# Output projection of block 1: seven products in place of eight, with the sums of its weights on GpSimd

## The reference

```python
def first_block(x, w_in, attn_sinks, conv_w, w_branch_a, w_branch_b, w_branch_c, w_out,
                ln1_g, ln1_b, w_ffn_gate, w_ffn_up, w_ffn_down, ln2_g, ln2_b):
    for l in range(DEPTH):
        mix = hybrid_mixer(x, w_in[l], attn_sinks[l], conv_w[l], w_branch_a[l],
                           w_branch_b[l], w_branch_c[l], w_out[l])
        x = layer_norm(ALPHA * x + mix, ln1_g[l], ln1_b[l])
        ffn = swiglu(x, w_ffn_gate[l], w_ffn_up[l], w_ffn_down[l])
        x = layer_norm(ALPHA * x + ffn, ln2_g[l], ln2_b[l])
    return x
```

## Time and profile before

| | |
|---|---|
| median of three runs | 2504.95 us (2500.95, 2504.95, 2506.22) |
| the profiled execution | 2509.21 us, span of its profile 2507.3 us |
| granted TensorE clock, mean over the span | 0.960 |
| TensorE matmuls busy | 2206.5 us (88%) |
| VectorE busy | 1181.2 us (47%) |
| ScalarE busy | 366.2 us (15%) |
| GpSimd busy | 38.5 us (2%), 69 instructions |
| HBM over the span | 262 GB/s |

### The profile page before, as it was taken

The page is one execution under the profiler, slowest core; times in us unless marked ns, Lnnn a source line. Parts: engine busy times, 40 slices in busy tenths (PEclk is TensorE's granted clock), DMA queues, the critical chain, the costliest instruction groups (busy, mean ns, idle before and its releaser), DMA issues.

```text
span 2507.3 us, 43433 instructions
## 1 busy us (share of the span) xinstructions
PE 2206.5 (88%) x19414; PEld 1567.8 (63%) x19414; DVE 1181.2 (47%) x2135; ACT 366.2 (15%) x818; POOL 38.5 (2%) x69
## 2 busy tenths in 40 slices
PE   8999999999999999999999988888799986555564
PEld 7898699488987984746545645454488643232322
DVE  6776477687755875935533221222435631111111
ACT  1121000012210000234521000000201520000000
POOL 0000000000000010000000000000000000000000
PEclk9999999999999999999998999999999998888877
DMA  8655755476558564511327999999921189999996
GB/s 318 223 167 200 242 183 213 154 252 236 168 185 268 169 222 162 199 45 36 118 111 331 418 427 426 426 427 425 377 103 34 71 339 425 427 426 428 427 427 282
DMA packets 168411, 659.15 MB, mean 263 GB/s; under 512 B 8326, under 2 KB 55938, under 8 KB 143522
## 3 DMA queue, kind: packets, MB, share of 16 engines
q1 hardware_dynamic: 162544, 639.66, 65.5%
q0 software_dynamic: 5312, 16.57, 2.1%
q10 hardware_dynamic: 370, 0.15, 0.0%
HBM read 655.12 MB, written 1.23 MB: 262 GB/s over the span
## 4 chain that ended last, share of the span: by engine, by line
PE 61%; DMA 29%; DVE 7%; ACT 2%; issue 1%; DVEq 0%; SPq 0%; ACTq 0%
PE psum L2291 21%; DMA ring<-in_moe_w_up 10%; DMA ring<-in_moe_w_gate 9%; DMA ring<-in_moe_w_down 9%; PE psum L789 5%; PE psum L2459 4%; PE psum L538 4%; PE psum L2236 3%; PE psum L2349 3%; PE psum L715 3%; PE psum L603 2%; PE psum L601 2%; PE psum L806 2%; PE psum L2467 1%; PE psum L2312 1%; PE psum L859 1%
## 5 line engine op out<-in xcount | busy, mean ns | idle before, releaser
L789 PE MATMUL psum<-ring,arena 128*32 128x256 f32 x5888 | 382.7, 416 | 161.8 <-DMA ring<-in_moe_w_up 87.3
L789 PEld LDWEIGHTS psum<-ring,arena 128*32 128x32 f32 x5888 | 207.8, 118 | 333.5 <-issue 138.3
L806 PE MATMUL psum<-ring,lnp 128*32 128x256 f32 x3072 | 193.9, 407 | 71.0 <-DMA ring<-in_moe_w_down 66.5
L1649 DVE TENSOR_TENSOR arena<-psum,spare 32x512 f32<-32x512 f32 (+1 forms) x128 | 70.9, 554 | 363.5 <-PE psum L806 362.2
L806 PEld LDWEIGHTS psum<-ring,lnp 128*32 128x32 f32 x3072 | 104.3, 116 | 158.4 <-DMA ring<-in_moe_w_down 50.5
L1638 DVE TENSOR_TENSOR lnp<-arena,psum 128x512 f32<-128x512 f32 (+1 forms) x32 | 26.1, 815 | 331.3 <-PE psum L789 331.3
L2291 PE MATMUL psum<-ht,ring 128*128 128x128 f32 x1408 | 168.2, 279 | 4.4 <-DMA ring<-in_w_in 3.4
L2291 PEld LDWEIGHTS psum<-ht,ring 128*128 128x128 f32 x1408 | 163.3, 195 | 8.4 <-issue 8.4
L538 PE MATMUL psum<-ring,ht 128*128 128x512 f32 x320 | 140.6, 595 | 0.0
L1096 ACT ACTIVATE arena<-psum 128x512 f32<-128x512 f32 (+1 forms) x32 | 15.7, 490 | 674.0 <-PE psum L789 674.0
L2693 DVE SCALAR_TENSOR_TENSOR spare<-ring,arena,spare 128x512 f32<-128x512 f32 x168 | 113.4, 743 | 0.0
(11 more groups left out here) (517 smaller groups left out, 3175.0 us busy)
## 6 DMA issues: line engine op xcount, KB each, us to landing
ring<-in_moe_w_down SPq DMA_DIRECT2D x64, 2048.0 KB
ring<-in_moe_w_gate SPq DMA_DIRECT2D x62, 2048.0 KB
ring<-in_moe_w_up SPq DMA_DIRECT2D x60, 2048.0 KB
ring<-in_w_in SPq DMA_DIRECT2D x52, 1024.0 KB
ring<-in_ada_w SPq DMA_DIRECT2D x48, 1024.0 KB
ring<-in_w_ffn_gate SPq DMA_DIRECT2D x22, 1024.0 KB
ring<-in_w_ffn_up SPq DMA_DIRECT2D x22, 1024.0 KB
ring<-in_w_ffn_down SPq DMA_DIRECT2D x20, 1024.0 KB
```

Source lines behind the costliest of these rows:

```text
L789: last = mm(bank[32 * j:32 * j + 32, SPLIT * m:SPLIT * m + SPLIT], (x_last if layer else x_four)[:, k, e % 4, SLOTS * m:SLOTS * m + SLOTS] ...
L806: last = mm(bank[32 * j:32 * j + 32, SPLIT * m:SPLIT * m + SPLIT], hidT[:, e % 2, a:a + 32], slot[:, f % 4, SPLIT * j:SPLIT * j + SPLIT], ...
L1649: ins = TTo(y_four[32 * q:32 * q + 32, s0:, cols], view(bank[r, 0:width], len(src), SPLIT), gb_moe[r, s0:, cols], ALU.mult)
```

## The change

The projection is taken as seven block products. With rows of `merged` (transposed) split in two halves of the inner dimension and tokens in two tiles, a11, a21, a12, a22 are blocks of 128 partitions x 4 x 128, and b11, b21, b12, b22 those of w_out, 4 x 512 columns each.

- TensorE: seven products of four calls, in the order 1, 6, 5, 2, 3, 7, 4, each with a bank; waits for the sums it needs.
- VectorE: four sums of `merged` blocks (128x512) after the merge. The assembly of the down projection is made into functions (`first_half`, `second_half`) and used for both; the weight sums of the first FFN panel now stand between the halves, behind a wait for GpSimd's last subtraction.
- GpSimd: four subtractions of w_out blocks (128x2048). They are queued ahead of the layer norm's parameter loads, wait for both w_out panels, for branch a's product (whose tiles they overwrite), for the merge of gate a, and the fourth for the last transpose of attention c.
- ScalarE: copies products 1 and 5 out of PSUM; the copy of `adaG` moves ahead of the first product of FFN panel 7 (counted from 0).
- Both w_out panels are released at the projection's end, where the first was released half way.

```diff
-    layer += [("wo", 0, 0), ("wo", 0, 1), R, ("wo", 1, 0), ("wo", 1, 1), R]
+    layer += [("wo", c) for c in SEVEN] + [R, R]
...
-        part_5 = ht[:, 3072:3584]
+        part_5 = [arena[:, 4608:5120], ht[:, 3072:3584]]
+        out_left = {5: view(arena[:, 3072:3584], 4, P), 6: view(arena[:, 3584:4096], 4, P), 3: view(arena[:, 4096:4608], 4, P)}
+        out_right = {6: view(ht[:, 2048:4096], 4, HALF), 7: view(arena[:, 10752:12800], 4, HALF), 4: view(arena[:, 0:2048], 4, HALF)}
...
+                for n_panel in (OUT_PANEL, OUT_PANEL + 1):
+                    pool.wait_ge(panel_in[n_panel % RING], l * (32 * LAYER_PANELS // RING) + 32 * (n_panel // RING + 1))
+                w1, w2 = (view(ring[:, n % RING, :], KT, HALF) for n in (OUT_PANEL, OUT_PANEL + 1))
+                b11, b21, b12, b22 = w1[:, 0:4, :], w1[:, 4:8, :], w2[:, 0:4, :], w2[:, 4:8, :]
+                sub = nc.gpsimd.tensor_tensor
+                pool.wait_ge(pe_done, banks.full("layer", ("ma", 3), l))
+                sub(out_right[7], b22, b12, ALU.subtract).then_inc(out_right_ready, 1)
+                pool.wait_ge(out_right_ready, 4 * l + 1)
+                sub(b12, b12, b11, ALU.subtract).then_inc(out_right_ready, 1)
+                pool.wait_ge(out_right_ready, 4 * l + 2)
+                pool.wait_ge(gate_a_merged, l + 1)
+                sub(out_right[6], b22, b12, ALU.subtract).then_inc(out_right_ready, 1)
+                pool.wait_ge(out_right_ready, 4 * l + 3)
+                pool.wait_ge(pe_done, banks.full("layer", ("ptc", 7), l))
+                sub(out_right[4], b21, out_right[6], ALU.subtract).then_inc(out_right_ready, 1)
                 pool.wait_ge(pe_done, banks.full("layer", ("sv", FIRST["ff"] - 1, "D"), l))
...
-                for n in range(2):
-                    project([("wo", n, 0), ("wo", n, 1)], panel(l, HALF), merged)
+                b1, b2 = panel(l, HALF), panel(l, HALF)
+                for c in SEVEN:
+                    bank = open_bank(pe, "layer", ("wo", c), l)
+                    if c in (5, 6, 3, 7):
+                        pe.wait_ge(out_left_ready, 4 * l + {5: 1, 6: 2, 3: 3, 7: 4}[c])
+                    if c in (7, 5, 6, 4):
+                        pe.wait_ge(out_right_ready, 4 * l + {7: 1, 5: 2, 6: 3, 4: 4}[c])
+                    for k in range(4):
+                        a = P * (c in (4, 7))
+                        left = out_left[c][:, k, :] if c in out_left else merged[:, 4 * (c in (2, 4)) + k, a:a + P]
+                        whole = b2 if c in (3, 5) else b1
+                        right = out_right[c][:, k, :] if c in out_right else whole[:, 4 * (c in (2, 3)) + k, :]
+                        last = mm(bank, left, right, start=k == 0, stop=k == 3)
+                    last.then_inc(pe_done, 1)
...
+                for c, part in ((1, part_1), (5, part_5[0])):
+                    take(("wo", c), part, part=HALF)
                 root(0, 0)
...
                 for p in range(PAIRS):
+                    if p == 7:
+                        take(("adaG",), ada_g, part=SEQ)
                     first_product(FIRST["ff"] + p)
...
+                            elif kind == "a" and m == 3:
+                                ins.then_inc(gate_a_merged, 1)
+                                dve.wait_ge(gate_a_merged, l + 1)
...
+                dve.wait_ge(merged_ready, l + 1)
+                a11, a21, a12, a22 = (merged[:, 4 * n:4 * n + 4, P * r:P * r + P] for n in range(2) for r in range(2))
+                TTo(out_left[5], a21, a22, ALU.add).then_inc(out_left_ready, 1)
+                dve.wait_ge(out_left_ready, 4 * l + 1)
+                TTo(out_left[6], out_left[5], a11, ALU.subtract).then_inc(out_left_ready, 1)
+                dve.wait_ge(out_left_ready, 4 * l + 2)
+                TTo(out_left[3], a12, out_left[6], ALU.subtract).then_inc(out_left_ready, 1)
+                TTo(a21, a11, a21, ALU.subtract).then_inc(out_left_ready, 1)
...
-                add_residual([("wo", 0, 0), ("wo", 0, 1)])
-                for t in range(TT):
-                    stats(t, (0,))
+                def first_half(kind):
+
+                    wait_emptied(dve, "layer", (kind, 1), l)
+                    scaled(x00, part_1)
+                    plus((kind, 6), part_12, part_1)
+                    for xs in (x01, x10, x11):
+                        scaled(xs, part_12)
+
+                def second_half(kind, n, loaded, done):
+
+                    wait_emptied(dve, "layer", (kind, 5), l)
+                    for xs in (x01, x11):
+                        step(TTo(xs, xs, part_5[n], ALU.add))
+                    plus((kind, 2), x00, x00)
+                    stats(0, (0,))
+                    plus((kind, 3), x01, x01)
+                    stats(0, (1,))
+                    layer_norm(n, 0, loaded, done)
+                    plus((kind, 7), x11, x11, last=False)
+                    stats(1, (1,))
+                    plus((kind, 7), x10, x10)
+                    plus((kind, 4), x10, x10)
+                    stats(1, (0,))
+                    layer_norm(n, 1, loaded, done)
+
+                first_half("wo")
+                dve.wait_ge(out_right_ready, 4 * l + 4)
                 weight_sums(FIRST["ff"])
-                add_residual([("wo", 1, 0)])
-                stats(0, (1,))
-                layer_norm(0, 0, ln1_loaded, x1_ready)
-                add_residual([("wo", 1, 1)])
-                stats(1, (1,))
-                layer_norm(0, 1, ln1_loaded, x1_ready)
+                second_half("wo", 0, ln1_loaded, x1_ready)
                 dve.wait_ge(x1_ready, 2 * l + 2)
```

More of the change, by code:

```diff
@@ L1895, in program @@
     LAYER_PANELS = banks.stage_panels["layer"][1]
-    ADA_PANELS, DOWN_PANEL = (5, 8, 13, 17, 21, 34), 39
+    ADA_PANELS, OUT_PANEL, DOWN_PANEL = (5, 8, 13, 17, 21, 34), 22, 39
     SEVEN_PANELS = (0, 1, 2, 6, 7, 10, 11, 14, 15, 18, 19, 27, 28, 29, 30, 31, 32, 33, 35, 36, 37, 38)
@@ L2032, in program @@
         gate_ready = sem("gate_ready")
+        gate_a_merged = sem("gate_a_merged")
+        out_left_ready, out_right_ready = sem("out_left_ready"), sem("out_right_ready")
         hid_sums_ready, w_sums_ready = sem("hid_sums_ready"), sem("w_sums_ready")
@@ L2587, in _ @@
                     A(ff[:, 0], ff[:, 0], ACT.Silu).then_inc(sil_ready, 1)
-                    if p == 7:
-                        take(("adaG",), ada_g, part=SEQ)
                 act.wait_ge(ctx_ms_ready, l + 1)
                 A(st[:, 4:6], st[:, 4:6], ACT.Sqrt).then_inc(ctx_rms_ready, 1)
-                for n, part in ((1, part_1), (5, part_5)):
+                for n, part in ((1, part_1), (5, part_5[1])):
                     take(("dn", n), part, part=HALF)
@@ L2831, in ada_columns, with scaled, plus @@
                     wait_emptied(dve, "layer", ("adaGT",), l)
[L2833 to L2839, removed]
+                dve.wait_ge(merged_ready, l + 1)
[6 more added lines that the diff above has]
+                TTo(a21, a11, a21, ALU.subtract).then_inc(out_left_ready, 1)
+                x00, x01, x10, x11 = (x[:, t, HALF * n:HALF * n + HALF] for t in range(TT) for n in range(2))
+                def scaled(xs, part):
+                    step(STT(out=xs, in0=xs, scalar=ALPHA, in1=part, op0=ALU.mult, op1=ALU.add))
+                def plus(key, out, xs, last=True):
+                    bank, freed = full_bank(dve, "layer", key, l)
+                    if last:
+                        TTo(out, xs, bank, ALU.add).then_inc(freed, 1)
                         wait_emptied(dve, "layer", key, l)
+                    else:
+                        step(TTo(out, xs, bank, ALU.add))
                 def stats(t, halves):
@@ L2964, in _ @@
                 V.reciprocal(ctx_rs, ctx_rs).then_inc(ctx_inv_ready, 1)
[L2965 to L2976, removed]
-                wait_emptied(dve, "layer", ("dn", 1), l)
-                scaled(x00, part_1)
-                plus(part_12, part_1, 6)
-                for xs in (x01, x10, x11):
-                    scaled(xs, part_12)
-                wait_emptied(dve, "layer", ("dn", 5), l)
-                for xs in (x01, x11):
-                    step(TTo(xs, xs, part_5, ALU.add))
-                plus(x00, x00, 2)
-                stats(0, (0,))
-                plus(x01, x01, 3)
-                stats(0, (1,))
-                layer_norm(1, 0, ln2_loaded, x_ready)
-                plus(x11, x11, 7, last=False)
-                stats(1, (1,))
-                plus(x10, x10, 7)
-                plus(x10, x10, 4)
-                stats(1, (0,))
-                layer_norm(1, 1, ln2_loaded, x_ready)
+                first_half("dn")
+                second_half("dn", 1, ln2_loaded, x_ready)
                 dve.wait_ge(x_ready, 2 * l + 4)
```

## The result

The changed kernel takes **2524.3 us** (median of four runs, 2521.7 to 2525.4) beside 2504.1 for the kernel before: ratio 1.0072, 95% interval 1.0057 to 1.0086 (the two medians alone give 1.0080). It is slower. The forecast, 2498.4, is wrong in size and direction, and the time lies 10.8 us above the range. Its profiled execution took 2524.78 us for a span of 2523.0.

What follows compares the result with a forecast made beforehand. TensorE bounds block 1, weight loads the expert stages. Per layer 3.45 us saved, about 0.1 taken back by VectorE: 2 x 3.3 = 6.6 us off the 2504.95 median gives 2498.4 us, own range 2496.5 to 2501, whole range to 2513.5.

Steps and rivals of the forecast that it cites:

- the one on GpSimd: Four weight subtractions per layer before the projection: GpSimd's reading beside VectorE was taken to cost VectorE nothing.
- rival 1: Before the second parts, GpSimd subtractions of g us each shut VectorE out: 3g - 6.4 us lost per layer; chance 0.30.
- GpSimd's price: Time of one 128x2048 subtraction: 3.8 us taken, between 2.3 and 4.6, from the ratio of one-column memsets.
- rival 2: Exclusion at the subtractions, but VectorE seldom yields: about 2.5 us delay a layer, net -0.8, 2503.3 us; chance 0.10.
- The product saved: Output projection on TensorE: seven products of four calls take 24.1 us, 3.45 us less per layer.
- VectorE's chain behind the projection: Assembly, FFN weight sums and layer norm after the projection: VectorE takes back about 0.1 us, leaving 3.3 gained per layer.
- Rival 3: VectorE's sums and assembly behind the projection run 1 us longer and bound it: 1 us lost per layer, 2500.4; chance 0.08.
- Rival 4: GpSimd's sums come too late for their readers, over 11.6 us each; at 14 us, 2517 in all; chance 0.04.
- Sums of the inputs: VectorE's four 128x512 sums after the merge, 0.69 us each, cost nothing: product 1 covers them.
- ScalarE's copies: Two bank copies of 0.60 us and the moved adaG copy of 0.36 us fall in ScalarE's idle time: nothing.
- the loads behind GpSimd: Layer norm parameter loads queued after the fourth subtraction land by 254, needed at about 278: nothing, 24 us of cover.
- Ring and SP queue: Later w_out releases and FFN panel loads cost nothing: the second panel's sums have 5.6 us of cover.

## Why the prediction was wrong, step by step

- **The step that failed** is the one on GpSimd: "What remains is what GpSimd's reading does to VectorE beside it: from below nothing, from above full exclusion (rival 1). I take nothing, because of the one stretch where GpSimd is busy beside VectorE". The row I took it from shows GpSimd issuing DMAs, which reads no tile, and I had called it weak myself. What the subtractions do is shut out VectorE's steps with SBUF operands while they run, which cost 7.45 us in layer 0 and 7.6 in layer 1. A row of the same engine with another kind of access is no row for this cost. In such a case the page (the Trainium skill, SBUF — State Buffer, "Who interferes with whom") was the better evidence, and the runs bear it out: the subtractions, which read, block two-input steps (5.00 us for 0.68), and fills don't touch them (4.05 us for six).
- **Rival 1 was the mechanism**, with place and pattern. It forecast 3g - 6.4; the measured g of 4.57 gives 7.3, measured 6.28. The waiting VectorE operation does get a turn between two subtractions, and so part of its work gets through. What the rival lacked is the clock: 1.2 us a layer, since TensorE comes back from 7 us of waiting at the lower level. The turns exclude rival 2: the three subtractions follow each other 0.08 us apart. They began at 223.56, 1.9 us later than the 222.2 read off the traffic (less the origin's 0.5), which changes nothing in the rival's sum.
- **GpSimd's price**: 3.8 us taken, 4.57 measured, near the upper end of 4.6 and near the 4.5 of the Trainium skill, GPSIMD Engine Reference, section 3.1. The ratio of two one-column memsets was a poor guide for 2048 columns.
- **The product saved** was right: 56 records, 3.43 to 3.53 us a product.
- **VectorE's chain behind the projection** was right in its own terms and lacked one: the panel that the sums read. I checked the second FFN panel's landing and not the first one's, whose cover the change took away (16.3 us to 9.9, against 12.3 to land). It cost 2.2 of the 3.3 us in layer 0, and VectorE 2.44 us of waiting in layer 1. Without it, with the panels swapped, 3.3 us are gained in both layers.
- **Rival 3** is the right form (over 0.5 us before tile 1's transposes, 1.91 measured in layer 0), for another reason than it gave. **Rival 4** is excluded: the fourth subtraction ended at 252.9, 12.9 us ahead of the projection.
- **Sums of the inputs, ScalarE's copies, the loads behind GpSimd** cost nothing, as said: no product waits between 265.81 and 290.1, and the parameter loads are issued at 252.81.
- **Ring and SP queue** I costed at nothing. TensorE's wait of 2.15 us among the ada products of layer 1 has no named cause; the kernel before has one of 0.73 us in layer 0. Such waits come and go from run to run and layer to layer. The early release took one away in layer 0 (1.63 us) and one of 0.78 us came in layer 1; by the ratios the step was worth 0.2%. Neither the cause nor a link to the release is shown.
- **The sum.** Per layer: 7.45 and 7.6 lost ahead of the projection. Behind it, up to the FFN's first product, layer 0 gains 2.27 us (36.43 before, 34.16 after), layer 1 loses 1.2. Together 14.0, less the origin's 0.5: 13.5, and 13.3 is read at the end of block 1. The spans' other 2.4 us and the medians' further 4.5 lie behind block 1 or between executions: the profiled executions of all twelve kernels, which have the same code there, took 1496 to 1505 us from L1209's operation to the end. That part stays open.

## What to carry to other kernels

Ask of every operation that is put on an "idle" engine which operands it reads, and which operations of the busy engine want the same path at that date. GpSimd at 3% and VectorE at 48% of the span still collided for 15 us, because both had their work at the same place; the same work timed into VectorE's PSUM reads and idle stretches cost TensorE nothing ahead of the projection (49.42 us again). And when a stage gets shorter, check for each of its loads not only that it is issued in time, but that it is still in by the earlier date of its reader.

## What the hardware showed that I had not expected

- GpSimd is not starved: beside back-to-back subtractions exactly one VectorE operation with SBUF operands passes per GpSimd operation (ends 228.41, 233.06, 237.98 against 228.13, 232.77, 237.42).
- The exclusion isn't of GpSimd's reads alone. A one-input VectorE TENSOR_SCALAR of 128x512, 0.43 us alone, is held by GpSimd subtractions (4.73) and by GpSimd fills (3.47 for two); the two-input step is held by subtractions only.
- A wait can cost more than its length. After 7.9 us almost without work the granted clock was 0.55 for 3.55 us; in layer 1 it read 0.52 from 799.0 to 801.6, behind the 2.15 us wait, and the eight transposes took 1.97 us where others take 1.06. Not every wait does this: behind the 1.91 us wait of layer 0 the clock read 1.00 and the eight took 1.09.
